# Attention scores and value products of two key heads in tiles of TensorE

## What is computed

```python
def sink_softmax(s, mask, sinks):
    s = jnp.where(mask, s, NEG_INF)
    sk = sinks.astype(jnp.float32)[:, :, None, None]
    m = jnp.maximum(jnp.max(s, axis=-1, keepdims=True), sk)
    p = jnp.exp(s - m)
    return p / (jnp.sum(p, axis=-1, keepdims=True) + jnp.exp(sk - m))

...
    q, k, v = swa_qkv(h, pos, w_qkv, q_norm, k_norm)
    qb = q.reshape(B, nb, SWA_BLOCK, SWA_KV_HEADS, SWA_GROUP, SWA_HEAD_DIM)
    kb = k.reshape(B, nb, SWA_BLOCK, SWA_KV_HEADS, SWA_HEAD_DIM)
...
    kk = jnp.concatenate([shift(kb), kb], axis=2)
    vv = jnp.concatenate([shift(vb), vb], axis=2)
...
    s = jnp.einsum('bnikgd,bnjkd->bnkgij', qb, kk).astype(jnp.float32) * (SWA_HEAD_DIM ** -0.5)
    p = sink_softmax(s, mask[None, :, None, None], sinks.reshape(SWA_KV_HEADS, SWA_GROUP))
    o = jnp.einsum('bnkgij,bnjkd->bnikgd', p.astype(vv.dtype), vv).reshape(B, T, SWA_Q_HEADS * SWA_HEAD_DIM)
    return o @ w_o, k[:, -WINDOW:], v[:, -WINDOW:]
```

## Time and profile before

| | |
|---|---|
| median of 3 runs | 3052.37 us |
| lowest, highest | 3050.44, 3052.54 us |
| span of the profiled execution | 3050.0 us |
| TensorE busy | 2976.0 us (98%) |
| VectorE busy | 1262.6 us (41%) |
| ScalarE busy | 742.6 us (24%) |
| GpSimd busy | 163.7 us (5%) |
| chain that ended last | 92% on TensorE, 5% on VectorE, 2% on ScalarE |
| mean granted TensorE clock | 0.989 of full speed |
| attention of the first pair, first scores to first output product | 97.9 us |

### The profile page before, as it was taken

How to read it: one execution, slowest core, us unless ns; L and a number is a source line. 1 busy time by engine, 2 the same in 40 slices (tenths; PEclk the granted TensorE clock), 3 DMA queues, 4 the chain that set the end, 5 groups by cost and what they waited for, 6 DMA issues and landing times.

```text
span 3050.0 us, 42635 instructions
## 1 busy us (share of the span) xinstructions
PE 2976.0 (98%) x17496; PEld 2777.9 (91%) x17496; DVE 1262.6 (41%) x1638; ACT 742.6 (24%) x1318; POOL 163.7 (5%) x78
## 2 busy tenths in 40 slices
PE   7999999999999999999999999899899999999999
PEld 7879959968986999999999999689679999999999
DVE  6443443443344633233332355744764233332333
ACT  3131132123123322111222131531553111222111
POOL 2000000000000200000000021211220000000000
PEclk9999999999999999999999999899899999999999
DMA  3122041122213111111111122103001111111111
GB/s 126 64 102 63 29 137 62 45 87 77 64 49 114 42 49 46 45 45 45 45 45 45 45 71 57 45 18 102 19 18 49 46 45 45 45 45 45 45 48 74
DMA packets 91333, 174.50 MB, mean 57 GB/s; under 512 B 9840, under 2 KB 15344, under 8 KB 90416
## 3 DMA queue, kind: packets, MB, share of 16 engines
q1 hardware_dynamic: 89296, 167.40, 17.1%
q10 hardware_dynamic: 1920, 5.41, 0.8%
HBM read 143.83 MB, written 25.56 MB: 56 GB/s over the span
## 4 chain that ended last, share of the span: by engine, by line
PE 92%; DVE 5%; ACT 2%; issue 1%; DMA 0%; ACTq 0%; SPq 0%; DVEq 0%
PE ps L1133 78%; PE ps L1298 2%; PE ps L1275 2%; PE ps L1470 2%; PE ps L1270 2%; PE ps L1444 1%; DVE wlo L701 1%; PE ps L1281 1%; PE ps L1173 1%; PE ps L1457 1%; PE ps L1304 1%; DVE x L738 1%; DVE hlo L708 1%; PE ps L1243 1%; ACT sq L477 1%
## 5 line engine op out<-in xcount | busy, mean ns | idle before, releaser
L1133 PE MATMUL ps<-hhi,whi 128*128 128x352 f32 x2976 | 651.0, 327 | 25.8 <-DVE hlo L708 16.3
L1133 PE MATMUL ps<-hhi,wlo 128*128 128x352 f32 x2976 | 643.5, 324 | 0.0
L1133 PE MATMUL ps<-hlo,whi 128*128 128x352 f32 x2976 | 643.0, 324 | 0.0
L468 ACT CAST whi<-wraw 128x512 fp32r<-128x512 f32 x424 | 261.1, 618 | 1135.2 <-PE ps L1133 1121.7
L701 DVE TENSOR_TENSOR wlo<-wraw,whi 128x512 fp32r<-128x512 f32 x424 | 333.9, 794 | 486.9 <-ACT whi L468 486.9
L1133 PEld LDWEIGHTS ps<-hhi,whi 128*128 128x128 f32 x2976 | 506.9, 190 | 29.7 <-DVE hlo L708 17.8
L1133 PEld LDWEIGHTS ps<-hhi,wlo 128*128 128x128 f32 x2976 | 512.7, 188 | 0.0
L1133 PEld LDWEIGHTS ps<-hlo,whi 128*128 128x128 f32 x2976 | 507.8, 189 | 0.0
L1133 PE MATMUL ps<-ahi,whi 128*128 128x352 f32 x2112 | 460.6, 326 | 9.1 <-DVE alo L1111 6.3
L1133 PE MATMUL ps<-ahi,wlo 128*128 128x352 f32 x2112 | 456.0, 323 | 0.0
L1133 PE MATMUL ps<-alo,whi 128*128 128x352 f32 x2112 | 455.3, 324 | 0.0
(11 more groups left out here) (156 smaller groups left out, 1925.0 us busy)
## 6 DMA issues: line engine op xcount, KB each, us to landing
wraw<-in_weights SPq DMA_DIRECT2D x424, 256.0 KB, 2.6
s<-in_state_in SPq DMA_DIRECT2D x32, 512.0 KB, 3.7
out_state_s<-s SPq DMA_DIRECT2D x32, 512.0 KB, 2.8
zr<-z_a ACTq DMA_DIRECT2D x40, 132.0 KB, 2.4
x<-in_xT SPq DMA_DIRECT2D x8, 528.0 KB, 8.7
rope_tab<-in_tables SPq DMA_DIRECT2D x4, 1056.0 KB, 4.8
out_yT<-x SPq DMA_DIRECT2D x8, 528.0 KB, 2.6
atab<-in_attn_tables SPq DMA_DIRECT2D x2, 1056.0 KB, 5.2
```

What stands on the lines that cost most here:

```text
L468: act.copy(whi[:, i % RING, :], wraw[:, i % RING, :]).then_inc(w_hi, 1)
L1133: mm = pe.matmul(ps[:, 3 * (m % 2) + t, 0:TB], a[:, slot, w], b[:, s * KG + k, t * TB:(t + 1) * TB], start=(first and j == 0), stop=(last ...
```

## The change

The keys are no longer padded: `k_a` holds both heads, each on its own 64 partitions, as the queries do. `block_scores(p, c)` now works on a block, for both heads: for each query head r it issues one matmul on partitions 0 to 63 (head 0, into banks 0 and 1) and one on partitions 64 to 127 (head 1, into banks 2 and 3). `block_out(p, c)` also works on a block: for each t one matmul with the 64 value features of head 0, whose result goes to partitions 0 to 63, and one with those of head 1, to partitions 64 to 127 of the same bank, 6 or 7 by the block's parity. In `pt_a` the slot that was for even or odd units is now head 0's or head 1's. The order on TensorE follows: scores come at odd k, for the two units k + 3 and k + 4; products come at even k, for the two units k - 2 and k - 1. `keep_out` copies a whole block with one instruction, at odd k. The new keys are turned once for both heads.

The diff, cut to its core:

```diff
@@ keep_out, on ScalarE @@
-            def keep_out(u, k):
-                rows = slice(HD * (k % 2), HD * (k % 2 + 1))
-                c = k // 2
-                act.wait_ge(pv_done, u + 1)
-                act.copy(q_a[rows, :, c * P:(c + 1) * P],
-                         ps[rows, 6 + k % 2, :].rearrange("p (r t) -> p r t", r=GR)).then_inc(out_kept, 1)
+            def keep_out(p, c):
+                act.wait_ge(pv_done, p * CH + c + 1)
+                act.copy(q_a[:, :, c * P:(c + 1) * P],
+                         ps[:, 6 + c % 2, :].rearrange("p (r t) -> p r t", r=GR)).then_inc(out_kept, 1)
@@ pair, on ScalarE @@
-                for s in range(2):
-                    col, f = s * P + s * HD, slice(s * HD, (s + 1) * HD)
-                    act.copy(nk[:, 0, f], ps[:, 7, col:col + HD]).then_inc(nk_kept, 1)
-                    act.copy(nk[0:NS, 1, f], ps[0:NS, 7, 2 * P + col:2 * P + col + HD]).then_inc(nk_kept, 1)
+                act.copy(nk[:, 0, :], ps[:, 7, 0:P]).then_inc(nk_kept, 1)
+                act.copy(nk[0:NS, 1, :], ps[0:NS, 7, P:2 * P]).then_inc(nk_kept, 1)
...
-                    if k >= 2:
-                        keep_out(u - 2, k - 2)
+                    if k >= 3 and k % 2:
+                        keep_out(p, (k - 3) // 2)
...
                     if k >= 2:
-                        act.wait_ge(pv_done, u - 1)
+                        act.wait_ge(pv_done, p * CH + k // 2)
                     act.copy(pt_a[:, u % 2, 1, :], ps[:, 5, :]).then_inc(pt1_kept, 1)
@@ finish_head and pair, on VectorE @@
-                if m < GR:
-                    dve.tensor_tensor(q_a[:, m, tok], z_a[:, m % 2, tok], wide_part(part), ALU.mult
-                                      ).then_inc(zq_done, 1)
-                else:
-                    for s in range(2):
-                        half = slice(HD * s, HD * (s + 1))
-                        dve.tensor_tensor(k_z[half, s, tok], z_a[half, m % 2, tok], wide_part(part)[half], ALU.mult
-                                          ).then_inc(zq_done, 1)
+                head = q_a[:, m, :] if m < GR else k_a
+                dve.tensor_tensor(head[:, tok], z_a[:, m % 2, tok], wide_part(part), ALU.mult).then_inc(zq_done, 1)
...
-                if p == 0:
-                    for s in range(2):
-                        dve.memset(k_z[HD * (1 - s):HD * (2 - s), s, :], 0.0).then_inc(kz_zero, 1)
...
                         dve.wait_ge(pt_done, turned(p, k) + 1)
-                        dve.wait_ge(pv_done, u - 1)
+                        dve.wait_ge(pv_done, p * CH + k // 2)
                         dve.tensor_copy(pt_a[:, u % 2, 0, :], ps[:, 4, :]).then_inc(pt0_kept, 1)
@@ block_scores and block_out, on TensorE @@
-            def block_scores(p, k):
-                u, c, s = p * HU + k, k // 2, k % 2
-                if k >= 2:
-                    pe.wait_ge(s_kept, u - 1)
+            def block_scores(p, c):
+                if c:
+                    pe.wait_ge(s_kept, p * HU + 2 * c)
...
                 for r in range(GR):
                     col = (r % 2) * 2 * P
-                    mm = pe.matmul(ps[:, 2 * s + r // 2, col + lo:col + 2 * P], q_a[:, r, c * P:(c + 1) * P],
-                                   k_z[:, s, keys], start=True, stop=True)
-                mm.then_inc(s_done, 1)
+                    for s in range(2):
+                        half = slice(HD * s, HD * (s + 1))
+                        mm = pe.matmul(ps[:, 2 * s + r // 2, col + lo:col + 2 * P], q_a[half, r, c * P:(c + 1) * P],
+                                       k_a[half, keys], start=True, stop=True)
+                        if r == GR - 1:
+                            mm.then_inc(s_done, 1)
...
-            def block_out(p, k):
-                u, c, s = p * HU + k, k // 2, k % 2
-                pe.wait_ge(pt1_kept, u + 1)
-                if k >= 2:
-                    pe.wait_ge(pt0_kept, p * (HU - 2) + k - 1)
-                    pe.wait_ge(out_kept, u - 1)
-                elif k == 1:
+            def block_out(p, c):
+                u = p * HU + 2 * c
+                pe.wait_ge(pt1_kept, u + 2)
+                if c:
+                    pe.wait_ge(pt0_kept, p * (HU - 2) + 2 * c)
+                if c >= 2:
+                    pe.wait_ge(out_kept, p * CH + c - 1)
+                elif c:
                     pe.wait_ge(os_kept, 2 * (p + 1))
                 for t in range(0 if c else 1, 2):
-                    mm = pe.matmul(ps[:, 6 + s, :], v_a[:, c - 1 + t, :], pt_a[:, u % 2, t, :],
-                                   start=(t == 0 or c == 0), stop=(t == 1))
+                    for s in range(2):
+                        half = slice(HD * s, HD * (s + 1))
+                        mm = pe.matmul(ps[half, 6 + c % 2, :], v_a[:, c - 1 + t, half], pt_a[:, s, t, :],
+                                       start=(t == 0 or c == 0), stop=(t == 1))
                 mm.then_inc(pv_done, 1)
@@ pair, on TensorE @@
                 for k in range(HU):
-                    if k + 3 < HU:
-                        block_scores(p, k + 3)
+                    if k % 2 and k + 3 < HU:
+                        block_scores(p, (k + 3) // 2)
                     if k == 3:
                         sample_out(p)
                     turn_probs(p, k)
                     if k == 2:
-                        pe.wait_ge(nk_kept, 4 * (p + 1))
+                        pe.wait_ge(nk_kept, 2 * (p + 1))
                         sample_turn(p)
-                    elif k == 3:
-                        block_out(p, 1)
-                        block_out(p, 2)
-                    elif k:
-                        block_out(p, k - 1)
-                block_out(p, HU - 1)
+                    if k and k % 2 == 0:
+                        block_out(p, k // 2 - 1)
+                block_out(p, CH - 1)
```

More of the change, by code:

```diff
@@ L156, in trunk @@
         q_a = at("q_a", o_work, [P, GR, TOK], F32)
-        k_z = at("k_z", o_work + 4 * TT, [P, 2, TOK], F32)
+        k_a = at("k_a", o_work + 4 * TT, [P, TOK], F32)
         o_a = o_work + 6 * TT
@@ L239, in trunk @@
         zs_done = sem("zs_done")
-        kz_zero = sem("kz_zero")
         av_turned = sem("av_turned")
@@ L315, in kept_before @@
         def kept_before(p):
-            return 18 * p
+            return 15 * p
         @block.sync
@@ L400, in _ @@
                                  ).then_inc(swa_out, 16)
-                sp.wait_ge(nk_kept, 4 * (p + 1))
+                sp.wait_ge(nk_kept, 2 * (p + 1))
                 sp.dma_start(kp_out[:, feats], nk[:, 0, :]).then_inc(swa_out, 16)
@@ L675, in pair @@
                                  ).then_inc(pts_kept, 1)
-                keep_out((p + 1) * HU - 2, HU - 2)
-                keep_out((p + 1) * HU - 1, HU - 1)
-                act.wait_ge(out_kept, HU * (p + 1))
+                keep_out(p, CH - 1)
+                act.wait_ge(out_kept, CH * (p + 1))
                 act.wait_ge(os_kept, 2 * (p + 1))
@@ L1374, in spread_tile @@
                 elif part == 2:
-                    pe.wait_ge(zq_done, kept_before(p) + (3 * m + 1 if m < GR else 3 * m + 2))
+                    pe.wait_ge(zq_done, kept_before(p) + 3 * m + 1)
                 spread(tile_use(p, m), part)
@@ L1412, in sample_scores @@
                     pe.matmul(ps[0:NS, 4 + b // 3, col:col + P], q_bd[:, b, :], kc[:, b, :], start=True, stop=True)
-                    for s in range(2):
-                        mm = pe.matmul(ps[0:NS, 4 + b // 3, col + P:col + KEYS], q_bd[:, b, :], k_z[:, s, SEQ:TOK],
-                                       start=(s == 0), stop=(s == 1))
+                    mm = pe.matmul(ps[0:NS, 4 + b // 3, col + P:col + KEYS], q_bd[:, b, :], k_a[:, SEQ:TOK],
+                                   start=True, stop=True)
                 mm.then_inc(sas_done, 1)
@@ L1495, in pair @@
                 pe.wait_ge(zq_done, kept_before(p + 1))
-                pe.wait_ge(kz_zero, 2)
                 block_scores(p, 0)
+                pe.transpose(ps[:, 7, 0:P], k_a[:, SEQ - P:SEQ], ident)
+                pe.transpose(ps[0:NS, 7, P:2 * P], k_a[:, SEQ:TOK], ident).then_inc(nk_done, 1)
+                sample_scores(p)
                 block_scores(p, 1)
-                for s in range(2):
-                    pe.transpose(ps[:, 7, s * P:(s + 1) * P], k_z[:, s, SEQ - P:SEQ], ident)
-                    mm = pe.transpose(ps[0:NS, 7, (2 + s) * P:(3 + s) * P], k_z[:, s, SEQ:TOK], ident)
-                mm.then_inc(nk_done, 1)
-                sample_scores(p)
-                block_scores(p, 2)
                 pe.wait_ge(sas_kept, 3 * (p + 1))
                 for k in range(HU):
-                    if k + 3 < HU:
-                        block_scores(p, k + 3)
+                    if k % 2 and k + 3 < HU:
+                        block_scores(p, (k + 3) // 2)
                     if k == 3:
```

## The result

The changed kernel takes 3057.85 us (median of 9 runs, 3053.4 to 3059.25) against 3051.66 for the kernel before (9 runs, 3046.47 to 3055.73): ratio 1.0021, 95% interval 1.0011 to 1.0030. It is slower, by about 6 us; the forecast was 14. The profiled execution spans 3056.1 us instead of 3050.0. In the code of after the names of the prediction stand at: S L1429, E L988, T L1443, C0 L1093, C1 L657, O L1459, K L611.

A forecast was written before the change was run, and what follows sets the result against it. TensorE was taken as the bound by 0.37 us a unit. Per pair keys -1.6, head -2.0, loops +6.7, tail +4.0 make +7.1; 3050.0 + 14.2 + 2.4 gives 3066 us, range 3044 to 3092.

The forecast's parts named there:

- S: Scores on TensorE; 1.73 us for a unit (a query block of one key head) before, forecast 1.94 for both heads.
- E: VectorE's reading that frees the scores' banks; forecast to start twice in about 9 to 11 us in the loop.
- T: The eight transposes of a unit on TensorE, 0.87 us; forecast a gap of about 3 us before each even unit's.
- O: Value products on TensorE; 1.72 us for a unit before, forecast 2.15 for both heads.
- K: ScalarE's copy of the result, 0.58 us; forecast that ScalarE no longer sits 13.11 us at that of unit 1.
- The bound and the series: Loop of two units: TensorE the bound before; then T, O, S and VectorE's work in series, 9.29 us against 8.65.
- Scores and products: S and O on TensorE: the two heads staggered by one record, 1.94 and 2.15 us.
- fully side by side: First rival, TensorE's part of the loop: halves run together, clock holds; loop 8.75, time 3042 to 3048 us; chance 0.15.
- The clock: Loop: TensorE's 3.1 us idle halves the granted clock for 3.2 us, 1.6 us late in each loop.
- The tail: From E of unit 14 to the first output product: +2.4 us, +4.0 with one drop of the clock.
- The head: First scores to E of unit 8: 1.2 and about 4 us gained, about 3 given back, -2.0 a pair.
- The keys: Ahead of the first scores: three whole key instructions instead of six on 64 partitions, -1.6 us a pair.

The follow-up runs named there:

- The two orders: Changed kernel with head 0's matmuls all before head 1's in S and O, 3073.1 us; with two matmuls of a head at a time in S, 3060.3 us.
- the keys alone: Kernel before with unpadded keys, new keys turned once, its order of work kept, scores on tiles of 64 rows: 3054.4 us, ratio 1.0005.
- The late O: Changed kernel with a second buffer of turned probabilities and block 0's O behind the sample's value products: 3067.2 us; 3054.0 with the buffer alone.
- the fills in the head: Changed kernel with filled loops (3040.9 us), plus unused full-array matmuls in three gaps of the head: 3040.6 us, ratio 0.9967.

## Why the prediction was right in sign and wrong in size

**The bound and the series: right.** TensorE's chain broke up into T, O, S and VectorE's work, with the gap ahead of T of an even unit (3.10 us; 3.1 was forecast), and the saving on TensorE bought nothing in the loop. At full clock the loop is 8.99 us; I had 9.29. The stagger of O, 0.28, is nearly all of the difference.

**Scores and products: the step failed, at small cost.** I held that a record which waits for its tile holds up those behind it. The two orders show that it does not as long as few wait. So O is 1.87, not 2.15, and S 1.93. That S met the forecast of 1.94 is luck: mine held a stagger of one record, with the change of tile counted apart, and the measured one holds the change of tile and no stagger. The measure is the rival's "fully side by side", with changes of tile that cost more than my 0.11: between S on half the rows and the full-array steps 0.15 and 0.19 each. The Trainium skill, page "TensorEngine Tiling (Array Packing)", section "Key Properties", has tiles load weights and multiply in parallel; these rows agree. Its page "TensorE: Matmul & The Clock Gate", section "Part 3: Packing small matmuls — row/col tiling", would have had the loads of O's two halves, which share their rows, stand between the matmuls; O at 1.87 for 8 records of 0.43, two at a time, leaves 0.15 for loads and change of tile together, so the trace disagrees again. The same section has matmuls start and end strictly in the order of issue; four records of 0.43 ahead of four others would then take at least 3.0 us, and O in that order took 1.87.

**The clock: right, and decisive.** A drop of 1.6 in each loop was forecast; the loops that lost the clock are 1.4 to 2.7 longer than the one that kept it, five of six did, and filling the gap gave all of it back. Over the six loops that is 1.5 each. Three loops came to +4.1 and +7.1 for +6.7, at mean clocks of 0.89 and 0.79, where 0.7 to 0.85 was forecast.

**The tail: right in its sum, by luck.** +5.0 and +3.9 for +4.0, but this was forecast as 2.4 of series and 1.6 of clock. With fills behind T of the odd units up to 13, at a clock of 0.99, it is +0.9: so the series costs 0.9 (the stagger of three O, 0.8, is about half of the difference) and the clock 4.1 and 3.0. Two errors cancel.

**The head: the step that made the miss.** I booked it at a rounded -2.0 (1.2 and 4 gained, 3 given back); it was -5.3 and -4.1. Up to E of unit 5 it gained 2.9 and 1.9, not 1.2. With the keys alone, 2.6 and 1.6 of that are there, and most of it is a term that my sum did not have: the first scores. Before, they ran at half clock in the first pair (3.54 us) and from about their middle on in the second (2.52); with the keys alone they ran at 1.00 (1.64), so 1.9 and 0.9 are theirs. TensorE's gaps just ahead of them are 1.13 and 1.47 us before, 0.41 and 0.35 there; that these gaps decide the clock is not shown. The single turning and copying of the new keys, for which I had booked the 1.2, is left with some 0.7. What is given back, O of block 0 ahead of E of unit 6, is 1.9, not 3. From E of unit 6 to E of unit 8 it gained 4.3 and 4.2, about the 4 of the forecast, though these are net of the series of T, O and S ahead of E of unit 8, which my 3 was to cover too. The late O shows the mechanism of this part: K waits again, and the head is longer. The parts do not add up exactly from run to run, since the clock falls in other places of the head each time: how much of the -5 belongs to the clock is not settled, and the fills in the head did not settle it.

**The keys: a little more than the -1.6.** From the start of the key instructions to the first scores it takes 1.53 us instead of 3.37 in either pair, -1.8, since three whole instructions take 1.38, less than half of 3.27. The -2.8 and -1.7 of the table cannot be told from scatter: the first scores of the other kernels, which leave the work ahead of them as it is in the changed kernel, start anywhere from 1905.5 to 1910.1, and 135.3 to 138.1 after the first pair's output products.

So of the miss of 8.1 us the head is 5.4, the loops 2.3, the keys and the scatter ahead of them 1.3; the tail was 0.9 worse than forecast.

## What to carry to other kernels

When two steps become one, ask for each engine what now stands in its queue ahead of the step that the next engine waits for. Here three orders kept the loop in series: S behind O, a copy that waits for O, K ahead of the exponentials. With only the copy's wait gone the loop was 9.0 at full clock, with only S moved 11.3 to 12.5, with both 9.0 to 10.3, and with all three 7.7; it was 8.65 before and 9.0 to 11.7 with the change. Other pairs of the three were not tried. And where TensorE is no longer the bound, price its idle pieces by the clock in the trace: the same gap can cost more than the work that was removed.

## What the runs showed of the hardware

- Two tiles of TensorE ran side by side with four-byte matmuls, two records and two loads each: 16 records of S in 1.93 us, where 8 took 1.73 on the full array and 1.92 on one tile of 64 rows alone. They did not start strictly in the order of issue: four records of one tile ahead of four of the other cost O nothing (1.87 us in both orders) and S 0.11, eight ahead of eight cost S 0.96.
- Narrowing the scores to 64 rows without a partner made each unit 0.34 us longer (4.66 instead of 4.32), though nothing was added: the two changes between half the rows and the full array took 0.19 (S) and 0.15 (T) more.
- Useless matmuls in a gap made a kernel 17 us faster. A gap of 3.1 us was followed by half clock in five of six loops, one of 1.2 to 1.8 in one of six, so a gap of this length is a risk, not a rule.
- The granted clock also fell while TensorE was busy, within the sample's value products of 32 columns: their 32 records took 6.6 us before (at 1.00 in the middle and 0.50 at either end), 9.0 in the kernel with the keys alone, at 0.50 throughout.
